# One decoder step on one core: the first norm taken tile by tile, the cached keys requested at the end of wv, and the second norm's weights applied where the gathered blocks leave PSUM

## The chip, the core and the metric

One core of a Trainium2 chip runs the whole program. The metric is the device time of one execution in microseconds. Engines are named as in the profile: PE (matrix), PEld (its weight loads), DVE (vector), ACT (scalar), POOL (GpSimd) and SP (which here only issues DMAs).

## The reference, cut to what matters

576 tokens (512 of a prompt, 64 sampled ones, 8 rows in each of 8 sequences) go through one layer with D = 1024.

```python
xn = rmsnorm(x, norm1_g)              # x * rsqrt(mean(x*x) + eps) * g
proj = xn @ w_in                      # u, v | rwkv r,k,v,w,a,g | q | 3 gates
mk_p, mv_p = mem_prompt @ xa_wk, mem_prompt @ xa_wv     # prompt's keys, values
o_xa = mem_attend(q, keys, values)    # samples use cache_mem_k, cache_mem_v
merged = sum over b of sigmoid(gate_b) * (o_b @ w_branch[b])
h = x + merged @ w_out
h = h + hier_moe(rmsnorm(h, norm2_g), ...)   # 32 experts, 2 for each token
y = rmsnorm(h, final_g)
# hier_moe: logits from the normed rows; expert(x) = (silu(x @ wg) * (x @ wu)) @ wd
```

The second norm's weight g multiplies column d of a row. It can be applied to the row at any place before the expert's first product, since the expert sees x * rstd * g.

## The kernel before, in words

Tokens lie in five tiles `TILES`: four of 128 rows and one of 64. Float32 products are made of three fp32r products: high times high, low times high, high times low.

**First norm (lines 1329 to 1343, 1963 to 1993, 2325 to 2351).** For each tile t ACT squares and sums the row and takes the root (`root(t)`), DVE takes the reciprocal and scales the row by it and by g (`normed(t)`, step "xn"), PE turns the tile in two halves of four 128x128 transposes (L1336), ACT copies each half out of PSUM as the high part (`high(t)`, L1977) and DVE subtracts it from PSUM for the low part (`rest(t)`, L2336). PE starts when `consts_ready` is set, which POOL does after all its constants (L2776). ACT and DVE take roots 0, 1, 2 first, then the high and low parts of tiles 0 and 1 between the roots of 3 and 4, then those of tile 2, then the weights of projection unit 0 (ACT makes their high part at L1960, DVE their low part at L2317, `upto(1, split)`), then tiles 3 and 4. PE waits for the last low part and for the unit's low weights, and then runs unit 0.

**Projection units.** `unit_plan` lists 45 units of weights: 7 "rwkv" units of 256 columns (0 to 6), u, v, q, wk, wv (15 and 16), 24 "merge" units and 4 "out" units (two of 512 output columns c, in two halves of the depth). SP loads each through a ring of four slots (`load_unit`); ACT and DVE split it in order. For a rwkv unit PE makes four parts: two blocks m of 128 output channels by two column ranges of tokens, 0 to 255 and 256 to 575; each part is 24 matmuls (L1412 to L1414). Between the first and the second part of unit 0 PE turns the previous rows (`shift_in`, L1384), which DVE copies out before it splits units 1 and 2.

**Queue of SP at the start (lines 1129 to 1149).** x tile 0, g1b (norm weights), x tiles 1, 2, 3, x tile 4, weights of unit 0, then the small tables and units 1 to 3.

**Cached keys (lines 1186 to 1210, 1827 to 1876).** SP, after the last wv unit has been evacuated by ACT, stores the prompt's values, loads unit 20, g2b (the second norm's weights on all partitions, 512 KB), seven small tables of the router, and then the 8 cached key blocks and 8 value blocks of 512 KB each through the six buffers `kvs`. PE turns the keys of block 0 (`turn_keys(0)`, L1836) after the probabilities of prompt tile 3 have been turned.

**The out stage and the router (lines 636 to 724, 793 to 917).** As DVE adds each tile's output to h (L707), ACT squares it (L666), PE turns it (L645) and makes the router's logits (L652). After the last h of half c, DVE multiplies h by g2b into x2 (`scaled(c)`, L697 and L699). At the end of the second half it does so before it takes the logits (L851). ACT scales x2 by rstd (L800) and stores it as `normed_tokens` (`x2_stored`). DVE then ranks the logits and writes `sel` (L886); PE counts places (L734, L736) and makes the lists (L744), with dummy products (`idle_products`, L620) between: 30 after the logits, 6 and 28 further on. POOL gathers each expert's rows by `il` (L980).

**The experts (lines 727 to 792, 809 to 935).** 32 experts, 64 rows each. For expert e PE turns the gathered block (`turn_in`, L751), ACT copies it to xs (L813), PE makes gate and up (L625, L626), ACT takes silu (L820), DVE multiplies (L924, "h"), PE turns that (`turn_h`, L778), DVE copies it (L934, "ht"), PE makes the down product (L632), DVE copies y (L929) and POOL scatters it (L989). PE's order is: gate_up(e), turn_in(e+1), down(e-1), turn_h(e). Each expert has 6 MB of weights in three slots of a ring of nine. SP's order is fixed: experts 0 and 1 and the gate weights of expert 2 as the out stage ends, the up weights of expert 2 (L589) after `x2_stored`, its down weights (L593) after the first two gathers, then each slot as an expert of three before has used it ("gh", "gu", "d").

## Time and profile before

| what | value |
|---|---|
| median of 3 runs | 1334.75 us (1333.68 to 1335.48) |
| the profiled execution, its own time | 1330.63 us |
| its span, first to last instruction | 1328.9 us |
| PE busy | 1184.9 us (89%) |
| PEld busy | 874.3 us (66%) |
| DVE, ACT, POOL busy | 410.0, 328.9, 92.8 us |
| mean granted TensorE clock | 0.961 |
| DMA moved | 283.80 MB |

The profiled execution is one of its own: 4.1 us under the median. Times of the trace are counted from the span's start. In the rows below a timeline line gives start, duration, engine, line, operation, written tile<-read tiles, count, and in brackets the engine's idle time before it with what ended it. Consecutive instructions of one line are merged, with their count.

### The profile page before, as it was taken

What the parts mean: (1) busy time and instruction counts of PE and PEld (TensorE: products, weight loads), DVE (VectorE), ACT (ScalarE), POOL (GpSimd) and SP (SyncE); (2) the same over time, 40 slices, a digit from 0 to 9 for tenths busy, and PEclk for the clock granted to TensorE, in tenths of its full rate; (3) what the DMA queues carried; (4) which work ended last, traced back from release to release, by engine and by line L of the source; (5) the groups of instructions that cost most, each with busy time, mean ns of one, the idle gap of its engine ahead of it and who ended that gap; (6) DMA issues with size and microseconds to landing.
All of it is one profiled execution on the core that took longest, in us unless ns stands there. A gap on an engine that the chain in (4) does not pass through costs nothing. (4 is left out here: it accounts for less than half of the span.)

```text
span 1328.9 us, 23704 instructions
## 1 busy us (share of the span) xinstructions
PE 1184.9 (89%) x10532; PEld 874.3 (66%) x10532; DVE 410.0 (31%) x705; ACT 328.9 (25%) x550; POOL 92.8 (7%) x132
## 2 busy tenths in 40 slices
PE   3999999999999989999999998999887778888870
PEld 3989998987789879999999877333332223333330
DVE  4336632243345534424233314111111111111116
ACT  5445232332432424223232313111000000010002
POOL 3000000000100010000000001111111111111100
PEclk8999989999899999999999999999999999998995
DMA  7110104000232572323232838999999999999976
GB/s 232 64 33 1 34 5 154 11 4 5 65 126 68 144 226 80 96 72 96 72 92 99 311 130 327 420 419 418 419 419 419 419 420 419 420 420 419 418 325 218
DMA packets 113281, 283.80 MB, mean 214 GB/s; under 512 B 23507, under 2 KB 70821, under 8 KB 88602
## 3 DMA queue, kind: packets, MB, share of 16 engines
q1 hardware_dynamic: 107402, 270.45, 53.9%
q0 software_dynamic: 5120, 9.46, 1.9%
q10 hardware_dynamic: 656, 2.36, 0.4%
q8 instruction: 84, 1.38, 0.4%
q14 instruction: 19, 0.16, 0.0%
HBM read 273.96 MB, written 15.60 MB: 218 GB/s over the span
## 5 line engine op out<-in xcount | busy, mean ns | idle before, releaser
L625 PE MATMUL bank<-slot,xs 128*64 128x512 f32 x512 | 248.6, 634 | 65.6 <-DMA slot<-in_e_wu_dram 64.4
L626 PE MATMUL bank<-slot,xs 128*64 128x512 f32 x512 | 249.8, 637 | 0.0
L625 PEld LDWEIGHTS bank<-slot,xs 128*64 128x64 f32 x512 | 69.7, 145 | 208.7 <-issue 207.2
L1243 PE MATMUL bank<-xnh,wh 128*128 128x256 f32 (+1 forms) x448 | 133.1, 297 | 0.6 <-DVE mt L2718 0.6
L1245 PE MATMUL bank<-xnh,low 128*128 128x256 f32 (+1 forms) x448 | 132.6, 296 | 0.0
L1244 PE MATMUL bank<-xnl,wh 128*128 128x256 f32 (+1 forms) x448 | 132.6, 296 | 0.0
L820 ACT ACTIVATE sg<-bank 64x512 f32<-64x512 f32 x32 | 19.0, 594 | 422.4 <-PE bank L626 422.4
L924 DVE TENSOR_TENSOR h<-sg,bank 64x512 f32<-64x512 f32 x32 | 21.7, 679 | 327.0 <-ACT sg L820 327.0
L632 PE MATMUL bank<-slot,ht 128*64 128x512 f32 x512 | 117.0, 598 | 0.5 <-DVE ht L934 0.5
L2317 DVE TENSOR_TENSOR low<-ring,wh 128x1536 fp32r<-128x1536 f32 (+1 forms) x45 | 89.9, 2005 | 84.4 <-ACT wh L1960 77.0
L1243 PEld LDWEIGHTS bank<-xnh,wh 128*128 128x128 f32 x448 | 85.0, 190 | 1.3 <-issue 1.2
L1960 ACT ACTIVATE wh<-ring 128x1536 fp32r<-128x1536 f32 (+1 forms) x45 | 75.4, 1682 | 41.3 <-PE bank L1294 20.8
L1244 PEld LDWEIGHTS bank<-xnl,wh 128*128 128x128 f32 x448 | 85.0, 190 | 0.0
L1245 PEld LDWEIGHTS bank<-xnh,low 128*128 128x128 f32 x448 | 85.0, 190 | 0.0
L632 PEld LDWEIGHTS bank<-slot,ht 128*64 128x64 f32 x512 | 34.1, 136 | 59.7 <-issue 50.2
L1412 PE MATMUL bank<-xnh,wh 128*128 128x256 f32 (+1 forms) x224 | 69.2, 309 | 4.2 <-DVE xnl L2336 4.2
L626 PEld LDWEIGHTS bank<-slot,xs 128*64 128x64 f32 x512 | 69.7, 145 | 0.0
L1413 PE MATMUL bank<-xnl,wh 128*128 128x256 f32 (+1 forms) x224 | 67.6, 302 | 0.0
L1414 PE MATMUL bank<-xnh,low 128*128 128x256 f32 (+1 forms) x224 | 67.5, 301 | 0.0
L1476 PE MATMUL bank<-sx 64*64 64x64 f32 x672 | 58.4, 227 | 7.4 <-issue 5.0
L1476 PEld LDWEIGHTS bank<-sx 64*64 64x64 f32 x672 | 55.5, 140 | 8.6 <-issue 6.0
L989 POOL DMA_INDIRECT expert_outputs<-yo,il x32 | 32.5, 1015 | 394.6 <-DVE ht L934 390.8
(477 smaller groups left out, 2230.9 us busy)
## 6 DMA issues: line engine op xcount, KB each, us to landing
slot<-in_e_wg_dram SPq DMA_DIRECT2D x64, 1024.0 KB, 28.4
slot<-in_e_wu_dram SPq DMA_DIRECT2D x64, 1024.0 KB, 28.0
slot<-in_e_wd_dram SPq DMA_DIRECT2D x64, 1024.0 KB, 28.7
ring<-in_w_in_dram SPq DMA_DIRECT2D x13, 1024.0 KB, 8.6
ring<-in_w_in_dram SPq DMA_DIRECT2D x24, 512.0 KB, 4.2
ring<-in_w_branch_dram SPq DMA_DIRECT2D x24, 256.0 KB, 4.7
kvs<-in_cache_mem_k_dram SPq DMA_DIRECT2D x8, 512.0 KB, 5.6
kvs<-in_cache_mem_v_dram SPq DMA_DIRECT2D x8, 512.0 KB, 4.4
```

Source lines behind the costliest of these rows:

```text
L625: pe.matmul(out[64:128, :], tok, wg[:, FF * k:FF * k + FF], start=(k == 0), stop=(k == KD - 1))
L626: mm = pe.matmul(out[0:64, :], tok, wu[:, FF * k:FF * k + FF], start=(k == 0), stop=(k == KD - 1))
L632: mm = pe.matmul(out[64 * c:64 * c + 64, :], hidden[:, f, :], wd[:, D * f + 512 * c:D * f + 512 * c + 512], start=(f == 0), stop=(f == 3))
L1243: pe.matmul(part, w_h, xh_(k, cols), start=(k == 0), stop=False)
L1244: pe.matmul(part, w_h, xl_(k, cols), start=False, stop=False)
L1245: mm = pe.matmul(part, w_l, xh_(k, cols), start=False, stop=(k == nk - 1))
L1412: pe.matmul(part, whi[:, w_], xnh[:, k, cols], start=(k == 0), stop=False)
L1413: pe.matmul(part, whi[:, w_], xnl[:, k, cols], start=False, stop=False)
L1414: mm = pe.matmul(part, wlo[:, w_], xnh[:, k, cols], start=False, stop=(k == KD - 1))
L1476: mm = pe.matmul(head2(2 * a, q, b), t[q, 1, b, :], t[q, 2, b, :], start=True, stop=True)
L1960: act.activation(unit_high(u), unit_raw(u), ACT.Copy).then_inc(hi_ready, 1)
L2317: dve.tensor_tensor(unit_low(u), unit_raw(u), unit_high(u).bitcast(F32), ALU.subtract)\
```

## The change

1. SP's queue at the start: unit 0's weights are asked for after x tile 2, ahead of x tiles 3 and 4. PE's transposes wait for a semaphore `ident_ready`, set as soon as POOL has made the identity. ACT's and DVE's orders take the high and low part of a tile one tile behind its root; unit 0 is split after tile 1. PE turns tiles 0 to 2, makes the two parts of unit 0 that need only tokens 0 to 255 (part m = 0, then turns tile 3, then m = 1, then turns tile 4), and the other two parts after the last low part, with `shift_in` between those.
2. The first four cached key blocks are asked for as soon as the last wv product is done, ahead of the store of the values, unit 20, and the small tables.
3. `scaled` is gone, g2b too. ACT scales h itself into x2. The weights g2x (128x2x4, two DMAs of 16-byte rows) multiply the gathered, turned block as it leaves PSUM, on DVE in place of ACT's copy; DVE does this for expert e+1 before it multiplies "h" of expert e. The branch for experts with over 64 rows is changed alike; it isn't entered here.

The diff, cut to its core:

```diff
-        act_n1 = Steps(... ("sq", 0) ... ("root", 2)] + both("hi", 0) + [("sq", 3), ("root", 3)] + both("hi", 1) ...
+        act_n1 = Steps(... ("root", 1)] + both("hi", 0) + [("sq", 2), ("root", 2)] + both("hi", 1) + [("sq", 3), ("root", 3)] ...
+        TURN_BANK = [0, 1, 2, 3, 4, 5, 6, 4, 5, 6]
...
-            def scaled(c):
-                dve_o.wait(dve, ("h", c, 4))
-                g = g2b[:, cols]
-                for m in range(2):
-                    dve.tensor_tensor(x2[:, 2 * m:2 * m + 2, cols], h[:, 2 * m:2 * m + 2, cols],
-                                      g.unsqueeze(1).to_broadcast([128, 2, 512]), ALU.mult)
-                dve_o.done(dve.tensor_tensor(x2[0:NS, 4, cols], h[0:NS, 4, cols], g[0:NS, :], ALU.mult), ("x2", c))
...
-                scaled(c)
...
             def gate_up(e):
-                act_e.wait(pe, ("xs", e))
+                dve_e.wait(pe, ("xs", e))
...
-            dve_o.wait(act, ("x2", OUTS - 1))
+            dve_o.wait(act, ("h", OUTS - 1, 4))
...
-                act_t.done(act.activation(x2[0:tn, t, :], x2[0:tn, t, :], ACT.Identity, scale=rstd[0:tn, t:t + 1]), ("x2", t))
+                act_t.done(act.activation(x2[0:tn, t, :], h[0:tn, t, :], ACT.Identity, scale=rstd[0:tn, t:t + 1]), ("x2", t))
...
-                act_e.done(act.activation(xs[e % 2][:, :, :], psum[2][:, :].rearrange("p (c n) -> p c n", n=128), ACT.Copy), ("xs", e))
...
+            def normed(to):
+                return dve.tensor_tensor(to[:, :, :].rearrange("p c (f n) -> p c f n", n=CAP),
+                                         psum[2][:, :].rearrange("p (c f n) -> p c f n", c=4, n=CAP),
+                                         g2x[:, :, :].rearrange("p f c -> p c f").unsqueeze(3).to_broadcast([128, 4, 2, CAP]), ALU.mult)
+
+            def evacuate(e):
+                pe_m.wait(dve, ("t", e))
+                if e >= 2:
+                    pe_m.wait(dve, ("gu", e - 2))
+                dve_e.done(normed(xs[e % 2]), ("xs", e))
+
+            evacuate(0)
             for e in range(EX + 1):
+                if e + 1 < EX:
+                    evacuate(e + 1)
                 if e < EX:
                     act_e.wait(dve, ("silu", e))
...
+                elif t == 2:
+                    load_units(0)
             sp.dma_start(x_sb[0:NS, 4, :], x_sample.rearrange("b t d -> (b t) d")).then_inc(x_loaded[4], 16)
-            load_units(0)
...
+            sp.wait_ge(unit_used, first_unit["wv"] + 2)
+            for n in range(4):
+                load_cache(n)
             act_evac.wait(sp, first_unit["wv"] + 1)
             store(mem_v_out[0, 0].rearrange("(m p) h d -> p m (h d)", p=128), vn[:, :, :])
             load_units(20)
-            sp.dma_start(g2b[:, :], norm2_g.to_broadcast([128, D])).then_inc(g2_loaded, 16)
+            for f in range(2):
+                sp.dma_start(g2x[:, f, :], norm2_g[0:1, 512 * f:512 * f + 512].rearrange("a (p c) -> (a p) c", c=4)).then_inc(g2_loaded, 16)
...
-            for n in range(2 * DB):
+            for n in range(4, 2 * DB):
...
-            pe.wait_ge(consts_ready, 1)
+            pe.wait_ge(ident_ready, 1)
+            for t in range(3):
+                turn_tile(t)
+            dve_n1.wait(pe, ("lo", 1, 1))
+            pe.wait_ge(lo_ready, 1)
+            rwkv_part(0, 0, 0)
+            turn_tile(3)
+            rwkv_part(0, 1, 0)
+            turn_tile(4)
             pe.wait_ge(par_loaded, 16 * 11)
...
             dve_n1.wait(pe, ("lo", 4, 1))
+            pe.wait_ge(consts_ready, 1)
...
-                if (u, n) == (0, 0):
+                if (u, n) == (0, 1):
                     shift_in()
...
+                    for n in range(2) if u else (1,):
+                        mm = rwkv_part(u, m, n)
...
-            for t in (0, 1, 2):
-                root(t)
-            for t in (3, 4):
-                high(t - 3)
-                root(t)
-            high(2)
-            upto(1, split)
-            for t in (3, 4):
-                high(t)
+            root(0)
+            root(1)
+            high(0)
+            root(2)
+            high(1)
+            upto(1, split)
+            root(3)
+            high(2)
+            root(4)
+            high(3)
+            high(4)
```

DVE's order is changed in the same way: normed 0, 1, rest 0, normed 2, rest 1, split of unit 0, normed 3, rest 2, normed 4, rest 3, rest 4. `rwkv_part(u, m, n)` holds the 24 matmuls of one part as before; `turn_tile(t)` the eight transposes of a tile, in the banks of TURN_BANK.

## Rows read from the trace of the kernel before

**Rows 1.** The page, part 2: busy tenths in 40 equal slices of the span

```profile
PE   3999999999999989999999998999887778888870
DMA  7110104000232572323232838999999999999976
```

**Rows 2.** Timeline of the first 45 us: ACT, DVE and PE

```profile
6.80 1.28 DVE L2329 SCALAR_TENSOR_TENSOR x_sb<-x_sb,rstd,g1b 128x1024 f32<-128x1024 f32 x1
7.91 1.06 ACT L1969 ACTIVATE xq<-x_sb 128x1024 f32<-128x1024 f32 x1 [1.59 <-DMA x_sb<-in_x_prompt_dram]
9.29 1.04 ACT L1969 ACTIVATE xq<-x_sb 128x1024 f32<-128x1024 f32 x1
13.80 4.24 PE L1336 MATMUL bank<-ident,x_sb 128*128 128x128 f32 x24 [13.80 <-POOL restart L2776]
14.95 0.60 ACT L1977 ACTIVATE xnh<-bank 128x512 fp32r<-128x512 f32 x1 [4.20 <-PE bank L1336]
20.96 1.91 ACT L1960 ACTIVATE wh<-ring 128x2048 fp32r<-128x2048 f32 x1
22.99 2.27 DVE L2317 TENSOR_TENSOR low<-ring,wh 128x2048 fp32r<-128x2048 f32 x1
27.18 0.58 PE L1412 MATMUL bank<-xnh,wh 128*128 128x256 f32 x1 [4.18 <-DVE xnl L2336]
31.64 1.03 PE L1384 MATMUL bank<-ident,shn 8*128 8x8 f32 x14
32.60 0.42 PE L1412 MATMUL bank<-xnh,wh 128*128 128x320 f32 x1
33.95 4.49 DVE L2317 TENSOR_TENSOR low<-ring,wh 128x2048 fp32r<-128x2048 f32 x2
...
42.62 0.28 PE L1412 MATMUL bank<-xnh,wh 128*128 128x256 f32 x1
```

**Rows 3.** DMA issues from 4.1 to 4.3 us (unit 0's weights): count, KB, us to landing

```profile
ring<-in_w_in_dram SPq DMA_DIRECT2D x1, 1024.0 KB, 12.2
```

**Rows 4.** PE's transposes of x_sb by stretch: us, busy (count), PEclk, DMA share, GB/s

```profile
14.30:14.80 0.50, 0.50 (x4) 1.00 1.15 283
16.80:17.30 0.50, 0.50 (x7) 1.00 1.05 320
```

**Rows 5.** All engines by stretch: PE, PEld, DVE, ACT, POOL busy, PEclk, DMA share, GB/s

```profile
28.00:30.00 2.00, 2.00 (x11) 2.00 (x11) 0.00 (x0) 2.00 (x2) 0.00 (x0) 0.50 0.01 0
...
812.00:813.00 1.00, 1.00 (x8) 1.00 (x6) 0.00 (x0) 0.00 (x0) 0.00 (x0) 0.51 1.06 434
824.00:825.00 1.00, 0.63 (x4) 0.44 (x4) 0.00 (x0) 0.33 (x1) 0.00 (x0) 1.00 0.00 0
```

**Rows 6.** Timeline of PE and SP around the cached keys

```profile
455.67 1.89 PE L1811 MATMUL bank<-ktm,o_xa 128*128 128x256 f32 x8
...
467.98 8.90 SPq L1210 DMA_DIRECT2D kvs<-in_cache_mem_k_dram  x8
...
472.58 1.09 PE L1836 MATMUL bank<-ident,kvs 128*128 128x128 f32 x8 [2.96 <-DMA kvs<-in_cache_mem_k_dram]
```

**Rows 7.** Timeline from the end of the out stage to the first gather

```profile
798.47 1.67 PE L652 MATMUL bank<-wr,hT 128*128 128x36 f32 x16
810.95 0.59 PE L734 MATMUL bank<-sel,before 128*128 128x192 f32 x2 [3.92 <-DVE sel L886]
...
798.89 2.35 DVE L697 TENSOR_TENSOR x<-h,g2b 128x1024 f32<-128x1024 f32 x2
...
802.15 0.30 DVE L851 TENSOR_TENSOR lg<-lg,bank 128x144 f32<-128x144 f32 x1
...
819.07 1.25 POOL L980 DMA_INDIRECT xg<-normed_tokens,il  x1 [19.91 <-DVE pg L909]
```

**Rows 8.** Timeline of the experts: PE's down product and DVE's product beside it

```profile
842.13 3.65 PE L632 MATMUL bank<-slot,ht 128*64 128x512 f32 x16
...
842.19 0.68 DVE L924 TENSOR_TENSOR h<-sg,bank 64x512 f32<-64x512 f32 x1 [7.23 <-ACT sg L820]
```

More of the change, by code:

```diff
@@ L550, in build @@
                                       ("sq", 4), ("ht", 4)]])
[L551 to L552 removed]
+        dve_o = Steps(sem("dve_o"), ["wr"] + [x for c in range(OUTS) for x in [("h", c, t) for t in range(5)] + ([("lg", c)] if c < OUTS - 1 else [])])
         pe_t = Steps(sem("pe_t"), ["pos", "lists"])
@@ L785, in moe_pe @@
                 if e + 1 < EX:
-                    act_e.wait(pe, ("xs", e))
+                    dve_e.wait(pe, ("xs", e))
                     turn_in(e + 1)
@@ L1043, in general_act @@
                         r = MORE * e + j
-                        pe_n.wait(act, "t", r)
-                        act_n.done(act.activation(xs[0][:, :, :], psum[2][:, :].rearrange("p (c n) -> p c n", n=128), ACT.Copy), "xs")
                         pe_n.wait(act, "gu", r)
@@ L1326, in units_of, with turn_tile, rwkv_part @@
                         unit(u)
-            pe.wait_ge(consts_ready, 1)
-            for n, (t, g) in enumerate(TG):
+            def turn_tile(t):
                 dve_n1.wait(pe, ("xn", t))
-                if n >= 7:
-                    dve_n1.wait(pe, ("lo", *TG[n - 7]))
-                tn = TILES[t][1]
-                for k in range(4):
-                    mm = pe.transpose(psum[n % 7][:, 128 * k:128 * k + tn],
-                                      x_sb[0:tn, t, 512 * g + 128 * k:512 * g + 128 * k + 128], ident[0:tn, 0:tn])
-                pe_n1.done(mm, ("turned", t, g))
+                t0, tn = TILES[t]
+                for g in range(2):
+                    n = 2 * t + g
+                    if n >= 7:
+                        dve_n1.wait(pe, ("lo", *TG[n - 3]))
+                    for k in range(4):
+                        mm = pe.transpose(psum[TURN_BANK[n]][:, 128 * k:128 * k + tn],
+                                          x_sb[0:tn, t, 512 * g + 128 * k:512 * g + 128 * k + 128], ident[0:tn, 0:tn])
+                    pe_n1.done(mm, ("turned", t, g))
+            PARTS = (slice(0, 256), slice(256, NT))
+            def rwkv_part(u, m, n):
+                whi, wlo = wh[:, u % 3, :], low[:, u % 4, :]
+                cols = PARTS[n]
+                part = rwkv_pair(u, m)[:, n, 0:cols.stop - cols.start]
+                for k in range(KD):
+                    w_ = slice(256 * k + 128 * m, 256 * k + 128 * m + 128)
+                    pe.matmul(part, whi[:, w_], xnh[:, k, cols], start=(k == 0), stop=False)
+                    pe.matmul(part, whi[:, w_], xnl[:, k, cols], start=False, stop=False)
+                    mm = pe.matmul(part, wlo[:, w_], xnh[:, k, cols], start=False, stop=(k == KD - 1))
+                return mm
+            pe.wait_ge(ident_ready, 1)
[7 more added lines that the diff above has]
+            turn_tile(4)
             pe.wait_ge(par_loaded, 16 * 11)
@@ L1402, in _ @@
                 pe.wait_ge(lo_ready, u + 1)
-                whi, wlo = wh[:, u % 3, :], low[:, u % 4, :]
                 for m in range(2):
@@ L2336, in rest @@
                     dve_n1.done(dve.tensor_tensor(xnl[:, 4 * g:4 * g + 4, t0:t0 + tn],
-                                                  psum[(2 * t + g) % 7][:, :].rearrange("p (k n) -> p k n", n=128)[:, :, 0:tn],
+                                                  psum[TURN_BANK[2 * t + g]][:, :].rearrange("p (k n) -> p k n", n=128)[:, :, 0:tn],
                                                   xnh[:, 4 * g:4 * g + 4, t0:t0 + tn].bitcast(F32), ALU.subtract), ("lo", t, g))
-            for t in (0, 1, 2):
-                normed(t)
-            for t in (3, 4):
-                rest(t - 3)
-                normed(t)
+            normed(0)
+            normed(1)
+            rest(0)
+            normed(2)
+            rest(1)
+            upto(1, split)
+            normed(3)
             rest(2)
-            upto(1, split)
-            for t in (3, 4):
-                rest(t)
+            normed(4)
+            rest(3)
+            rest(4)
             act_n1.wait(dve, "par")
@@ L2751, in _ @@
             seq(pool.memset(ident[:, :], 0.0))
-            select(ident[:, :], [[-1, 128]], 0, 1, ALU.not_equal, 1.0)
+            pool.affine_select(out=ident[:, :], in_=ident[:, :], compare_op=ALU.not_equal, fill=1.0, base=0, pattern=[[-1, 128]],
+                               channel_multiplier=1).then_inc(ident_ready, 1)
             seq(pool.memset(i64[:, :], 0.0))
```

61 lines of the change are left out of this document (24 added, 37 removed).

## The prediction

> **What bounds the kernel now.** I read the page's slices first. PE is busy nearly without a break from the second slice to the 24th (800 us), and in these slices the DMA line stands mostly at 0 to 5; from the 26th slice (830 us) it is the other way round, DMA at 9 and PE soon at 7 or 8 [rows 1]. So up to the end of the out stage every microsecond of idle PE is one of the total; in the expert stage the weights' stream sets the pace, and what counts is when that stream runs without a pause and how much of the tail follows it. A change can gain in three places: before PE's first product, in a hole of PE before 800 us, and between the end of PE's stage and the full stream. The change touches one of each.
>
> Then I read the timelines of these places. At the start PE waits 13.80 us for POOL's last constant though the first normed tile is there at 6.80 + 1.28 = 8.08; it turns tiles, waits again 4.18 us for the last low part, and starts unit 0 at 27.18 [rows 2]. Around the cached keys PE has one hole of 2.96 us, ended by the landing of the first key block [rows 6]. At the turn to the experts DVE takes the logits at 802.15, though PE has them at 798.47 + 1.67 = 800.14: the multiplication by the norm's weights (2.35 us for the four full tiles, from 798.89) stands between. PE then idles 3.92 us for `sel`, and the first gather goes out at 819.07 [rows 7].
>
> **The start.** SP asks for unit 0's weights before x tiles 3 and 4, so they land no later than the 4.15 + 12.2 = 16.35 us of before [rows 3]; with 0.75 MB fewer ahead I take 12 to 14. ACT's new chain in order: square and root of tile 1 from 7.91 (a tile takes 1.4, from one square at 7.91 to the next at 9.29) to 9.4; high part of tile 0, two times 0.60, which finds PE's transposes just done (they need 14.95 - 13.80 = 1.15 to the first half, now from 8.1); tile 2's root to about 12.2; high part of tile 1 to 13.4; high part of unit 0, 1.91, to 15.4. DVE's low part of unit 0 takes 2.27, to about 17.8 [rows 2]. DVE's own norms and low parts fit in between: a norm is 1.28.
>
> PE starts part 0 there. The part has 24 matmuls. On the fast clock the last three parts of unit 0 took 42.62 - 32.60 = 10.0 for 320 + 256 + 320 columns, so one of 256 takes 2.9 and one of 320 takes 3.6. On the slow clock it takes about 4.5: the first part took 31.64 - 27.18 = 4.46, most of it at granted clock 0.50 (1.2 GHz) [rows 2, 5]. I take slow for the first and fast for the second. So: 17.8 + 4.5 = 22.3, tile 3's eight transposes 1.4 (a third of 4.24), second part 2.9 to 26.6, tile 4 and the tables' transposes 1.2 (estimate from the same row), the last high and low parts 1.1: PE is free to go on at 28.9. What is left is 3.6 + 1.03 (`shift_in`) + 3.6 = 8.2 against 42.62 - 27.18 = 15.4 from the old start. Unit 0 ends at 37.1 instead of 42.6: **5.5 us less**. Moved instructions cost nothing beyond that: SP issues the same DMAs, POOL nothing new.
>
> What is late next is unit 1's low part. It is ready 33.95 + 4.49/2 = 36.2, so 3.5 after the end of `shift_in` at 32.67 [rows 2]; now only one part of 3.6 lies behind `shift_in`. A tie: 0 to 0.2.
>
> The ends: with unit 0's weights no earlier than 16.35, the low part comes at 20.7, 2.9 later, and the gain is 2.6; with both parts on the fast clock PE goes on at 27.0 and the gain is 7.4 (1.6 more from part 0, the rest from faster transposes).
>
> Which clock? The granted clock stands at 1.00 from the first instant, before any PE work, but the pace tells otherwise: PE does 4 transposes in half a microsecond at 14.3 and 7 at 16.8 [rows 4]. So it began slow and sped up while it ran nothing but transposes. In the new order the transposes come in three bursts with pauses, which is why I take slow for the part behind them. The Trainium skill, TensorE: Matmul & The Clock Gate (PE-mode transpose), says that transposes don't count as busy for the clock. Rows 4 speak against that for these ones. By that rule the first part is slow for certain (5.5); by rows 4 it may be fast (7.4).
>
> **The cached keys.** They are asked for at 467.98 and land 4.6 later, at 472.58 less the hand-over; PE was ready 2.96 earlier, at 469.6 [rows 6]. Now they are asked for when the last wv product ends, about 455.8 (the scores that follow it start at 455.67), and land at 460 to 462 with the other three: 8 us of slack, and unit 20 and the small tables, which now go behind 2 MB, aren't used for 20 us and more. Blocks 4 and up still wait for steps of PE that move with it. **2.9 us less**; between 2.5, if the copies of the first turned keys are late by some tenths, and 2.96. Two tiny loads in place of one of 512 KB: nothing, SP has time there.
>
> **The turn to the experts.** Without `scaled`, DVE takes the logits at 800.2 instead of 802.15: 1.95 less, not the whole 3 us, because PE's logits are then late next. `scaled` of the first half lies beside PE's work and is worth 0. `sel` comes 1.95 earlier, and PE's 30 dummy products are done before (807.0), so PE idles 1.97 instead of 3.92 [rows 7]. After the long idle time the granted clock fell to 0.51 at 812 [rows 5], and PE's matmuls for places and lists run in that stretch. If it doesn't fall any more, the chain to the gather gains about 1.0 again (estimate: some 0.4 in the counting products and 0.6 in the six dummy products that then end before DVE). Both are about as likely; I take the middle, 2.5. The gather also needs `x2_stored`. ACT starts on x2 2.3 earlier, but these writes share the DMA with expert weights, so I expect them 1 to 2 earlier, which is enough. Against it stands the copy of the gathered block, 0.60 on ACT for 128x512 [rows 2], now on DVE: nearest row 0.68 for 512 columns with a PSUM operand [rows 8]; 0.1 once, at expert 0. **2.4 us less**; ends 0 (below) and 2.9.
>
> That the stream of weights gives this on to the end: DMA moves nothing at 824 to 825 [rows 5], so it waits for this chain and there is idle time to remove.
>
> In each expert DVE now does the block for e+1 before "h" of e. Waiting behind it: h, and PE's `turn_h`. Before, h was ready at 842.19 + 0.68 = 842.9 and PE's down product held until 842.13 + 3.65 = 845.8 [rows 8]: 2.9 of cover for 0.7. Only expert 0 has no down product before; it is late by 0.7, behind the first releases of slots, and costs nothing while the stream has work queued. Without that cover it would cost 0.7 once.
>
> **Sum.** 5.5 + 2.9 + 2.4 = 10.8. The profiled execution took 1330.63, so it would be 1319.8; it lies 4.1 under the median. I take the same 10.8 off the median: 1334.75 - 10.8 = 1324.0.
>
> **Rivals.**
> A. Unit 0's weights come as late as before, because their small rows and not their place set the landing. The start gives 2.6, the total 7.9: 1326.9. For it: they took 12.2 us for 1 MB. Against: 0.75 MB and more of x went ahead. 0.17.
> B. The turn to the experts gives nothing, because x2's writes and the weights already fill the DMA (share 1.06 at 812) and the first gather waits for `x2_stored`. Total 8.4: 1326.4. Against: DMA at 0.00 at 824. 0.10.
> C. The clock is kept in both places. 7.4 + 2.9 + 2.9 = 13.2: 1321.6. For it: rows 4. 0.16.
> D. Slower. DVE's product with the broadcast weights in a 4-level pattern takes far over 0.7. From 2.9 on it stalls PE at `turn_h` in every expert; PE has, at 7 to 8 tenths busy, some 3 us of waiting in each expert to give away. So it decides from about 6 us, and from 6.4 on (31 experts by 0.4) the gain is eaten and the kernel is slower by over 0.2%, at 1338 for 6.45. No row has such a price. 0.02.
> E. Two of the three parts are worth nothing, for instance by a new wait of PE for unit 1's low part and a late `x2_stored`; a total under 2.7. 0.05. That the change doesn't do what it says belongs here: the experts' stage is shortened by 3 us on DVE in the text, but only 2 can count.
>
> The forecast itself has 0.50. About 0.2% (2.7 us) is what a measurement of this kernel can tell from no change. All but D and E are faster: 0.93, same 0.05, slower 0.02. The range goes from C, with 1 us for the spread of medians, to A and B together (5.5 less): 1320.5 to 1329.2.
>
> **What would show it.** Right: part 0 starts near 18 us and unit 1 near 37; no hole before L1836, which starts near 464 (472.6 less 5.5 and 2.9); L851 right behind the logits; the hole before L734 near 2 us; DMA full some 10 to 11 us earlier; DVE's new product at 0.7. Wrong: unit 0's high part waiting for a DMA after 14 us; a wait of PE for unit 1; a gather that waits for `x2_stored`; a hole in the DMA share around experts 1 to 3.

## The result, and the profile after

The changed kernel takes 1322.46 us (median of 4 runs, 1321.68 to 1323.27); the kernel before, run beside it, takes 1335.12 (1333.68 to 1335.73). The ratio is 0.9913, 95% interval [0.99, 0.9925]: 12.7 us less. The profiled execution took 1323.27 with a span of 1321.5, so it is 7.4 shorter than the profiled execution of before, which was one of the short ones. A second set on another chip gave 0.9925 [0.9912, 0.9939], 9.8 us less by the medians.

Part 2 of the page of the changed kernel, busy tenths in 40 slices, against [rows 1]:

```profile
PE   6999998999999999999999997999877888878870
DMA  7210105000322662232323758999999999999976
```

The first slice of PE went from 3 to 6. At the other end the DMA line looks as it did: the stream of the weights has its 9 in the same slices of a shorter span.

The start, from the timeline of the changed kernel (start us, us, engine, line, operation, and in brackets the idle time before it with what ended it), against [rows 2]:

```profile
8.16 1.94 PE L1341 MATMUL bank<-ident,x_sb 128*128 128x128 f32 x8 [8.16 <-DVE x_sb L2354]
13.37 1.90 ACT L1983 ACTIVATE wh<-ring 128x2048 fp32r<-128x2048 f32 x1
15.31 2.29 DVE L2342 TENSOR_TENSOR low<-ring,wh 128x2048 fp32r<-128x2048 f32 x1 [0.50 <-ACT wh L1983]
17.75 0.55 PE L1353 MATMUL bank<-xnh,wh 128*128 128x256 f32 x1 [2.10 <-DVE low L2342]
20.23 0.41 PE L1355 MATMUL bank<-xnh,low 128*128 128x256 f32 x1
21.98 1.03 PE L1341 MATMUL bank<-ident,x_sb 128*128 128x128 f32 x8
27.54 0.41 PE L1353 MATMUL bank<-xnh,wh 128*128 128x320 f32 x1 [0.65 <-DVE xnl L2361]
35.91 0.39 PE L1353 MATMUL bank<-xnh,wh 128*128 128x256 f32 x1
```

Part 0 starts at 17.75 (17.8 was forecast). ACT takes the weights at 13.37 with no wait for a DMA: they are there. Part 0 is slow up to 20.45 (a product every 0.21 us) and fast from then on (every 0.12). The granted clock in the rows of this stretch reads 1.00 throughout, so slow and fast are told here by the pace of the products. Unit 1 starts at 35.91 instead of 42.62.

The cached keys, same timeline, against [rows 6]:

```profile
449.62 1.89 PE L1834 MATMUL bank<-ktm,o_xa 128*128 128x256 f32 x8
449.82 1.91 SPq L1187 DMA_DIRECT2D kvs<-in_cache_mem_k_dram  x4
463.41 1.04 PE L1859 MATMUL bank<-ident,kvs 128*128 128x128 f32 x8
```

They are asked for at 449.82, the hole is gone, and PE turns them 9.17 us earlier than before, 6.05 of which were there already at the scores (455.67 to 449.62).

The turn to the experts, same timeline, against [rows 7]:

```profile
788.75 1.67 PE L652 MATMUL bank<-wr,hT 128*128 128x36 f32 x16
790.51 0.30 DVE L832 TENSOR_TENSOR lg<-lg,bank 128x144 f32<-128x144 f32 x1 [0.59 <-PE bank L652]
799.31 0.59 PE L724 MATMUL bank<-sel,before 128*128 128x192 f32 x2 [1.99 <-DVE sel L867]
805.20 0.80 SPq L576 DMA_DIRECT2D slot<-in_e_wu_dram  x2
806.75 1.25 POOL L975 DMA_INDIRECT xg<-normed_tokens,il  x1 [17.31 <-DVE pg L890]
814.40 0.75 PE L741 MATMUL bank<-ident,xg 128*128 128x128 f32 x4 [3.19 <-DMA xg<-normed_tokens,il]
815.18 0.69 DVE L901 TENSOR_TENSOR xs<-bank,g2x 128x512 f32<-128x512 f32 x1 [7.74 <-PE bank L741]
821.32 0.33 SPq L576 DMA_DIRECT2D slot<-in_e_wg_dram  x1
```

Up to the gather all goes as intended. In this text a time counted from the logits is counted from the start of the last row of sixteen logits' products (788.75 here, 798.47 in the kernel before). That row comes 9.72 earlier than before; DVE takes the logits 0.09 behind its end (790.42); the gather goes out at 806.75, so 12.32 earlier: the chain gained 2.60. Then it is lost. PE waits 3.19 for the gathered block and turns it at 814.40; in the kernel before this was at 823.88, so only 9.48 are left. And from the logits to the first slot that SP may fill again it is 821.32 - 788.75 = 32.57 us, where the kernel before needs 829.01 - 798.47 = 30.54: 2 us more. What that is worth at the end is taken up with the experiments.

The stretches of the changed kernel (PE, PEld, DVE, ACT, POOL busy with counts, PEclk, DMA share, GB/s), against [rows 5]:

```profile
804.00:806.00 2.00, 2.00 (x31) 1.86 (x30) 0.70 (x4) 0.00 (x0) 0.00 (x0) 1.00 0.04 14
806.00:812.00 6.00, 5.21 (x47) 5.02 (x45) 1.24 (x9) 1.49 (x2) 2.25 (x2) 1.00 0.98 362
813.00:815.00 2.00, 0.60 (x4) 0.56 (x4) 0.00 (x0) 0.00 (x0) 0.00 (x0) 1.00 0.03 12
816.00:819.60 3.60, 3.60 (x10) 1.10 (x12) 0.00 (x0) 0.00 (x0) 0.92 (x1) 0.53 0.92 380
```

The clock no longer falls where it fell before [rows 5]; it falls now behind the wait for the gathered block, and the first half of expert 0's gate and up products runs at 1.2 GHz (granted clock 0.53). While the gather is under way the DMA is full (0.98), and it stands idle before and behind that (0.04 and 0.03). What fills it are the up weights of expert 2, which SP asked for 1.55 us before the gather, in the row of 805.20. They are two DMAs of 1 MB, so 2 MB; the expectations below call this load, and that of the gate weights, 1 MB, which is half of it. In the kernel before, SP asked for them at 814.86, 4.21 before the gather.

The DMA issues of this stretch, changed kernel first, then the kernel before (count, KB each, median us from issue to landing; the gather is the first one alone):

```profile
normed_tokens<-x ACTq DMA_DIRECT2D x4, 512.0 KB, 9.8
xg<-normed_tokens,il POOLq DMA_INDIRECT x1, 7.6
```

```profile
normed_tokens<-x ACTq DMA_DIRECT2D x4, 512.0 KB, 7.4
xg<-normed_tokens,il POOLq DMA_INDIRECT x1, 4.8
```

ACT starts on the normed tokens 1.21 us behind the start of the logits' last row (789.96) and not 3.68 behind it (802.15), but their writes take 2.4 longer beside the same weights, so SP's up weights go out 16.45 us behind the logits, as before (16.39). The chain to the gather moved, the weights ahead of it did not.

Behind the first release something else is new. PE waits for expert 0's `h`, its multiplication on DVE, first in the changed kernel, then in the one before (PE's timeline):

```profile
826.76 0.69 PE L768 MATMUL bank<-ident,h 64*128 64x64 f32 x4 [1.37 <-DVE h L919]
```

```profile
833.81 0.69 PE L778 MATMUL bank<-ident,h 64*128 64x64 f32 x4 [0.73 <-DVE h L924]
```

DVE does the block of expert 1 first, so `h` comes 0.64 later, and expert 1 releases its first slot 9.76 behind expert 0's (at 831.08) and not 9.11. Twice the DMA runs dry before the weights that a release allows are under way: its share is 0.46 in 821.75 to 822.75 and 0.66 in 833.75 to 834.75. The kernel before has no such place in the same stretch.

### The profile page after: what moved, and what is told of

Read it like the earlier page. It is cut to its first block and busy times, and to the rows that moved or that the text cites. A ratio compares the mean times of both kernels' runs of the same rounds, so it can differ in the third digit from the quotient of the medians.

```text
span 1321.5 us, 23698 instructions
## 1 busy us (share of the span) xinstructions
PE 1184.7 (90%) x10532; PEld 874.2 (66%) x10532; DVE 423.4 (32%) x731; ACT 310.3 (23%) x518; POOL 93.3 (7%) x132
## 5 line engine op out<-in xcount | busy, mean ns | idle before, releaser
L901 DVE TENSOR_TENSOR xs<-bank,g2x 128x512 f32<-128x512 f32 x32 | 22.1, 692 | 322.1 <-PE bank L741 322.1
```

## The experiments

Executions of one kernel differ by up to some 4 us to either side of their median, so each kernel was timed in 5 to 12 executions beside the kernel before, and the profiled execution of each was read by stages. The table gives the length of each stage in us, each the difference of two starts in the timelines: *start* is the first product of unit 1; *middle* goes from there to the first turned probabilities; *to keys* to the first turned keys; *behind keys* to the last turned probabilities of the cached part; then the out stage, up to the logits, is 291.30 to 291.33 in all and is left out; *routing* goes on to the issue of the first gather; *block* to the first slot that SP fills again; *stream* to the first load of the tail. The last column is the sum of the three before it.

| kernel | start | middle | to keys | behind keys | routing | block | stream | last three |
|---|---|---|---|---|---|---|---|---|
| before | 42.62 | 414.78 | 15.18 | 34.56 | 20.60 | 9.94 | 471.82 | 502.36 |
| before again | 43.17 | 416.10 | 15.99 | 36.01 | 21.44 | 9.71 | 471.81 | 502.96 |
| start only | 36.88 | 416.75 | 16.24 | 36.18 | 20.53 | 10.45 | 471.85 | 502.83 |
| keys only | 43.52 | 416.87 | 12.06 | 34.40 | 20.81 | 10.18 | 471.88 | 502.87 |
| second norm only | 43.75 | 416.95 | 14.39 | 34.22 | 19.23 | 13.19 | 471.66 | 504.08 |
| keys' hole filled | 42.98 | 419.40 | 16.00 | 34.37 | 22.04 | 9.67 | 472.29 | 504.00 |
| changed | 35.91 | 415.44 | 12.06 | 34.04 | 18.00 | 14.57 | 472.39 | 504.96 |
| changed again | 37.05 | 417.19 | 12.06 | 33.88 | 18.00 | 14.31 | 472.33 | 504.64 |
| parts 1 and 2 | 37.39 | 414.03 | 12.07 | 33.60 | 20.58 | 10.51 | 471.77 | 502.86 |
| gather first | 36.03 | 415.03 | 12.06 | 34.10 | 18.01 | 9.42 | 477.27 | 504.70 |
| 42 dummies | 36.05 | 415.53 | 12.06 | 33.49 | 19.16 | 12.54 | 472.03 | 503.73 |
| gate weights later | 37.23 | 414.10 | 12.07 | 33.62 | 18.01 | 14.50 | 471.27 | 503.78 |
| the same, more dummies | 36.87 | 417.09 | 12.07 | 33.91 | 18.01 | 14.11 | 471.74 | 503.86 |
| weights behind gather | 35.96 | 415.41 | 12.06 | 33.81 | 20.55 | 14.59 | 472.09 | 507.23 |

**The start alone**: the kernel before with the pieces of the diff on `act_n1`, `dve_n1`, `TURN_BANK`, `ident_ready`, `load_units(0)`, `turn_tile` and `rwkv_part`.

> Part 1 alone (the first norm tile by tile). Theory: all of the start's gain is made before unit 1, whose first product starts at 35.9 us instead of 42.6, and about 0.7 of it is given back before the cached keys, as the profile of the whole change shows; the rest reaches the end. About 6.0 us less: ratio 0.9955. Rival: the gain is worth more than the profile shows (the medians of the two kernels lie 12.7 apart, the profiled executions 7.4), then this part is at 8 or more, ratio under 0.994.

Measured: 1327.71 us (6 runs), ratio 0.9941 [0.992, 0.9962]. Unit 1 starts at 36.88; the hole before the keys is still there. PE's timeline at the keys:

```profile
469.87 1.96 PE L1857 MATMUL bank<-ident,kvs 128*128 128x128 f32 x8 [4.01 <-DMA kvs<-in_cache_mem_k_dram]
471.62 2.77 PE L1864 MATMUL bank<-prt,vn 128*128 128x128 f32 x16
```

The hole is 4.01 and not 2.96, and behind it eight transposes take 1.96 us and sixteen products 2.77: the clock fell in the hole (granted clock 0.52 in the first microsecond behind it, 0.50 in the next two). In the profiled execution of the kernel before it had not (1.00 there, and 1.09 for the transposes [rows 6]).

**The keys alone**:

```diff
+            sp.wait_ge(unit_used, first_unit["wv"] + 2)
+            for n in range(4):
+                load_cache(n)
             act_evac.wait(sp, first_unit["wv"] + 1)
...
-            for n in range(2 * DB):
+            for n in range(4, 2 * DB):
```

> Part 2 alone (the first four cached key blocks asked for at wv's end). Theory: PE's hole of 2.96 before L1836 goes, and 0.1 to 0.5 of the wait for the last value block with it: 3.1 us less, ratio 0.9977. Rival: the time goes into a later wait, ratio within 0.0005 of 1.

Measured: 1328.85 (6 runs), ratio 0.9953 [0.9936, 0.9969]: some 6 us less, at least 4, where 2.9 was forecast. The profile shows no hole and fast transposes:

```profile
472.45 1.04 PE L1841 MATMUL bank<-ident,kvs 128*128 128x128 f32 x8
```

**The second norm alone**: the remaining pieces of the diff (`g2x`, `normed`, `evacuate` on DVE, `scaled` gone).

> Part 3 alone (the second norm's weights at the evacuation). Theory from the profile of the whole change: the logits are taken 2.0 earlier and the gather goes out 2.6 earlier, but it lands late, since the up weights of expert 2 go out just before it; the first expert starts no earlier, on a slow clock, and the weights' stream is full 2 us later than it could be. The kernel is 0 to 2 us slower, ratio 1.000 to 1.0015. Rival from the medians: what is left of 12.7 after 6.0 and 3.1 is this part's, so 3 us faster, ratio 0.9975, and the late gather is seen in this one profile alone.

Measured: 1334.02 (12 runs), ratio 0.9994 [0.9981, 1.0007]: no gain that can be seen. The interval goes from 2.5 us less to 0.9 more, so by the timed runs alone neither the 2.4 of the prediction is ruled out nor a small loss. Timeline of this kernel (PE, SP, POOL):

```profile
817.14 0.80 SPq L575 DMA_DIRECT2D slot<-in_e_wu_dram  x2
819.86 1.25 POOL L974 DMA_INDIRECT xg<-normed_tokens,il  x1 [18.55 <-DVE pg L889]
826.12 0.75 PE L740 MATMUL bank<-ident,xg 128*128 128x128 f32 x4 [1.80 <-DMA xg<-normed_tokens,il]
```

The same picture with nothing else changed: the up weights stand 2.72 ahead of the gather, a new hole of 1.80 stands before the block, and from the logits to the first release it takes 19.23 + 13.19 = 32.42.

**The kernel before once more**, as a measure of what an execution differs by.

> The kernel before, unchanged, profiled and timed once more. Theory: the profiled execution of before (1330.6) was one of the shortest that this kernel has, and most take 1334 to 1336; then this profile shows 3 to 5 us more in a place that can be named, most likely the landing of the first gathers and the clock behind it. Rival: a profiled execution is always some 4 us shorter than the others; then this one is near 1331 too, with the same times at all places.

Measured: 1333.11 (12 runs), ratio 0.9994 [0.9979, 1.0008]. PE at the keys in this execution:

```profile
475.26 1.78 PE L1836 MATMUL bank<-ident,kvs 128*128 128x128 f32 x8 [3.76 <-DMA kvs<-in_cache_mem_k_dram]
```

Here too the clock fell in the hole (granted clock 0.62, then 0.50). Of the four profiled executions with the late keys and an open hole, the clock fell in the two with holes of 3.76 and 4.01 and stayed in the two with 2.96 and 2.16. By the table the late keys cost (15.45 - 12.06) + (35.24 - 33.87) = 4.8 us on average, from these four against the nine with early keys. By these profiles it is 4.8 that part 2 gives, not the 2.96 of one execution.

**The keys' hole filled**, to see whether the second half of that cost is the clock. The keys stay late:

```diff
             def turn_keys(b):
+                if b == 0:
+                    act_x.wait(pe, ("p", 3))
+                    for _ in range(26):
+                        pe.transpose(psum[SKT_BANK[0]][:, 0:128], ident[:, :], ident[:, :])
                 pe.wait_ge(kv_loaded[b % KVS], 16 * (b // KVS + 1))
```

> The kernel before with 26 dummy transposes of the identity in the hole ahead of the first turned keys; the keys are asked for as late as before. Theory (in most executions of the kernel before the hole is 3.5 to 4 us, and the clock falls in it, which costs 1.5 to 2 us more than the hole): PE has almost no idle time ahead of the keys, the eight transposes take 1.1 us instead of 1.8, the sixteen products behind them 1.95 instead of 2.94, and the total is 1 to 2 us below the kernel before: about 0.9988. Rival (the hole alone is the cost): 1.000, and the transposes behind it are as slow as they were.

PE's timeline of this kernel at the keys:

```profile
474.44 3.00 PE L1831 MATMUL bank<-ident 128*128 128x128 f32 x26
478.38 1.09 PE L1840 MATMUL bank<-ident,kvs 128*128 128x128 f32 x8 [0.94 <-DMA kvs<-in_cache_mem_k_dram]
```

In the profile it does what was expected: 16.00 to the keys, so the hole without the dummies would be 3.9, and the transposes take 1.09. *Behind keys* is 34.37, not the 36.0 of the two executions with a slow stretch. In the medians nothing is seen of it: 1333.98 (11 runs), ratio 1.0001 [0.9992, 1.001], where 0.9988 was expected. So the fall in the hole is shown in traces, and its price of 1.6 when it happens; that it happens in most executions is not borne out. By the interval the clock's part is at most 1.1 us, so the late keys cost 3.4 to 4.5 in the median by this run, and at least 4.1 by the run with the keys alone; the table's average is 4.8. The price stays open to that extent.

**The changed kernel again**, beside the next runs.

> The changed kernel again, beside the next three on the same chip. Both theories: 0.9905 of the kernel before (12 to 13 us less); the first gathered block lands 7 to 8 us after it is asked for, the transposes of the gathered block wait some 3 us for it, the first half of the first expert's gate and up products runs at 0.85 us for a pair instead of 0.43, and the first slot is released some 14.5 us after the gather was asked for.

Measured: 1324.22 (5 runs), 0.9925 [0.9912, 0.9939]. The gather is followed by the turned block 7.43 later, after a wait of 2.96, and by the first release 14.31 later; all as before.

**The gather ahead of the weights**:

```diff
             dve_t.wait(sp, "lg")
             sp.wait_ge(x2_stored, 80)
-            load(2, 1)
             dve_t.wait(sp, "c12")
             for n in range(2):
                 sp.wait_ge(gathered[n], 16)
+            load(2, 1)
             load(2, 2)
```

> The changed kernel with the up weights of expert 2 asked for only behind the landing of the first two gathers. Theory (the gather is late because 1 MB of weights was queued 1.5 us ahead of it): it lands 4 to 5 us after it is asked for, so 3 us earlier; PE's wait for it (3.2) is gone, the clock does not fall, and the first slot is released 3 to 4.5 us earlier than in the changed kernel. The total: 2 to 4 us less than the changed kernel if the weights' stream passes this on; 0 if the 1 MB that now starts later is missed, which would be seen as a wait of PE for the weights of expert 2. Rival (the gather is slow by itself: small rows, normed_tokens written just before): it still takes 7 us, nothing gained, and the 1 MB asked for 8 us later makes it 1 to 3 us slower.

The timeline of this kernel (POOL, PE, SP) from the gather on:

```profile
806.54 1.25 POOL L975 DMA_INDIRECT xg<-normed_tokens,il  x1 [17.32 <-DVE pg L890]
810.84 0.64 PE L741 MATMUL bank<-ident,xg 128*128 128x128 f32 x4
811.61 0.81 SPq L576 DMA_DIRECT2D slot<-in_e_wu_dram  x2
815.96 0.33 SPq L576 DMA_DIRECT2D slot<-in_e_wg_dram  x1
```

The first half holds entirely: with no weights beside it the gather lands 3.5 us after its issue and is turned at 4.30, without a wait, and the first slot is released 9.42 after the issue, 5.1 earlier than in the changed kernel. The second half does not: the median is 1324.70, 0.9937 [0.9923, 0.9951], nothing gained. The stretches say why. First the changed kernel, from the logits to the first release, the 14 us behind it, and the first 50 us behind the logits; then the same of this one, then of the kernel before (columns as above):

```profile
788.75:821.32 32.57, 26.07 (x220) 21.31 (x220) 14.24 (x90) 9.00 (x13) 3.77 (x4) 0.95 0.84 327
821.32:835.32 14.00, 12.63 (x62) 4.94 (x60) 1.83 (x4) 1.19 (x2) 1.00 (x1) 1.00 0.92 349
788.75:838.75 50.00, 42.13 (x295) 27.20 (x293) 17.22 (x95) 10.19 (x15) 4.77 (x5) 0.97 0.87 339
```

```profile
788.53:815.96 27.43, 24.11 (x220) 20.82 (x220) 14.25 (x90) 9.00 (x13) 3.78 (x4) 1.00 0.72 276
815.96:829.96 14.00, 12.63 (x54) 4.58 (x52) 1.70 (x3) 0.59 (x1) 1.00 (x1) 0.88 1.01 421
788.53:838.53 50.00, 45.31 (x312) 28.63 (x312) 18.26 (x97) 10.19 (x15) 6.38 (x7) 0.97 0.85 341
```

```profile
798.47:829.01 30.54, 25.93 (x220) 22.53 (x220) 16.25 (x92) 9.59 (x14) 3.77 (x4) 0.94 0.84 321
829.01:843.01 14.00, 13.27 (x64) 5.08 (x62) 1.78 (x3) 2.38 (x4) 1.00 (x1) 1.00 1.02 423
798.47:848.47 50.00, 44.66 (x308) 29.65 (x308) 19.07 (x97) 11.97 (x18) 5.79 (x6) 0.97 0.91 360
```

Time by rate gives the bytes. From the logits to the tail all three move some 202.5 MB, and from 50 us on all run at 408 GB/s, so what counts is what the first 50 us moved: 339 by 50 = 17.0 MB in the changed kernel, 17.1 with the gather first, 18.0 before. The missing 1 MB is 2.5 us at 408 GB/s; by the last column of the table the changed kernel is 2.6 longer than the kernel before and the one with the gather first 2.3. The two lose it at different places. With the gather first the DMA is idle ahead of the first release (27.43 by 0.28 = 7.7 us, against 32.57 by 0.16 = 5.2 in the changed kernel) and full behind it (421). In the changed kernel it runs dry behind the release (349). So a release that came 5 us earlier gave nothing, because 2.5 us more of idle DMA were paid for it.

This holds for all fourteen profiles. From 50 us behind the logits on they run at 408 or 409 GB/s, and the bytes of the first 50 us order their last columns: 17.5 to 18.0 MB in the six with the old second norm (502.36 to 504.00 us), 17.0 to 17.3 in the seven others that end at 503.73 to 504.96, and 15.9 in the last kernel of the table (507.23).

**More dummy products** in the wait for the block (28 to 42 in `moe_pe`).

> The changed kernel with 42 instead of 28 dummy products ahead of the first gathered block. Theory (PE's idle 3.2 us ahead of the block make the clock fall, and the first half of the first expert's products pays 1.7 us for it): PE is busy until about 813, no pair of products takes 0.85, the first slot is released 1.7 us earlier, and the total is 1 to 1.7 us less than the changed kernel. Rival (the pace of these products does not count, since the stream is set by the landing of weights already under way): the first release comes earlier but the total is the same within 0.5.

Measured: 1322.07 (5 runs, 1318.08 to 1323.83), 0.9909 [0.9891, 0.9926], the fastest median and 2.1 below the changed kernel on the same chip, though the intervals overlap. The block's first release is 12.54 behind the gather instead of 14.31, and *last three* is 0.9 to 1.2 shorter. But this profile has slow stretches elsewhere, one ahead of the gather and one behind PE's wait for expert 0's `h` (granted clock 0.50 from 827 to 830). A row of its timeline, and the stretch behind it for the first of them (columns as above):

```profile
799.00 0.76 PE L724 MATMUL bank<-sel,before 128*128 128x192 f32 x2 [1.99 <-DVE sel L867]
```

```profile
800.00:802.00 2.00, 2.00 (x11) 2.00 (x10) 0.12 (x1) 0.00 (x0) 0.00 (x0) 0.50 1.02 418
```

The same idle time of 1.99 before the selection, behind which the changed kernel stayed at 1.00, ended here at 0.50, and the gather came 1.15 later.

**Parts 1 and 2 without the second norm.**

> The start and the keys as changed, the second norm as in the kernel before. By the profiles so far the stretch from the last logits product to the first store of the tail takes 502.4 to 503.0 us with the old second norm and 503.7 to 505.0 with the new one. Theory (the new second norm costs 1.5 us, since the gather now stands behind 1 MB of weights and the clock falls ahead of the first expert): this kernel is 0 to 1.5 us faster than the whole change, 0.990 to 0.9915 of the kernel before, with logits near 788.6, the gather asked for 20.5 later and the first slot released 31 us after the logits. Rival (the second norm is worth the 2.4 us of the prediction): 0.9925 to 0.994, slower than the whole change.

Measured: 1322.84 (6 runs), 0.9925 [0.9906, 0.9943]. By the median this is the changed kernel; the two can't be told apart. The stages of the profiles say that the third part is worth less than nothing: *last three* is 502.86, and over all, six profiles with the old second norm give 502.36 to 504.00 (mean 503.0), three with the new one and nothing else in that stage 504.08 to 504.96 (mean 504.6). The timed runs don't bear 1.6 us out: the interval of the second norm alone ends at 0.9 more. The timeline of this kernel (POOL, PE):

```profile
808.98 1.25 POOL L981 DMA_INDIRECT xg<-normed_tokens,il  x1 [19.89 <-DVE pg L910]
814.36 0.75 PE L752 MATMUL bank<-ident,xg 128*128 128x128 f32 x4 [0.57 <-DMA xg<-normed_tokens,il]
```

The up weights are asked for at 805.37. The gather goes out 2.2 later than in the changed kernel and its block is turned at the same time, 814.36 against 814.40.

**The gate weights of expert 2 behind the normed tokens**, to give their writes the DMA:

```diff
-            load(2, 0)
             dve_t.wait(sp, "lg")
             sp.wait_ge(x2_stored, 80)
+            load(2, 0)
             load(2, 1)
```

> The changed kernel, with the gate weights of expert 2 (1 MB) asked for right ahead of its up weights, so behind the landing of the normed tokens, and not ahead of them. Theory (the stream loses what the DMA stands idle between the landing of the normed tokens and the first slot's release, and the gather is late behind the up weights): the normed tokens land 2 to 3 us earlier, near 12 us after the logits instead of 16.5, both loads are issued there and nearly through when the gather is asked for, the gather lands in 4.5 to 6 us instead of 7.6, the first slot is released 1.5 to 5 us earlier with the rest of the stage as long as before (472 us), and the total is 2 to 4 us below the changed kernel: 0.988 to 0.990. Rival (the stage is set by bytes alone, and idle time of the DMA only moves): 0.9915 to 0.9925 as the changed kernel.

Measured: 1322.28 (6 runs), 0.9916 [0.9896, 0.9936]: as the changed kernel. A DMA issue and a row of the timeline of this kernel:

```profile
normed_tokens<-x ACTq DMA_DIRECT2D x4, 512.0 KB, 4.4
```

```profile
813.94 0.75 PE L741 MATMUL bank<-ident,xg 128*128 128x128 f32 x4 [3.15 <-DMA xg<-normed_tokens,il]
```

The writes do land in 4.4 instead of 9.8, and SP goes on 11.3 us behind the logits. But with 4 MB behind them instead of 2 the DMA is full until past 810, and the gather is late as before, turned 7.61 behind its issue. The expected 4.5 to 6 was wrong.

**The same with more dummies** (40 in the wait for the selection, 34 in that for the block):

> The same as the run before it, with 40 instead of 30 dummy products in the wait for the selection and 34 instead of 28 in the wait for the gather, so that the clock has no hole of 2 us to fall in. If the clock matters here: no stretch at 0.5 between the logits and the second expert, the gather 18.0 us after the logits in every execution, and 0 to 1.5 us less than the run before. If not: the same within 0.5.

Measured: 1322.71 (6 runs), 0.9917 [0.9898, 0.9936], no difference from the run before it. The hole before the selection is filled, but PE still waits 1.4 for the block, and the clock still falls behind it.

**The weights right behind the gather**: in the changed kernel, `load(2, 1)` one line down, behind `dve_t.wait(sp, "c12")`.

> The changed kernel with the up weights of expert 2 asked for at DVE's last step of the routing, some 0.8 us behind the issue of the first gather instead of 1.5 us ahead of it, and not behind its landing as in the run that loaded them behind the gathers. Theory (from the logits to the end the kernel moves the same bytes at the full rate, and what it loses is the idle time of the DMA in between; the gather is late by what was queued ahead of it): the gather lands in 4.3 to 5.2 us, the clock does not fall, the first slot is released 27.5 to 28.5 us after the logits, the rest takes 474 to 475 (472 plus the 1 MB that was not moved before), and logits to tail is 502 to 503 us, where the changed kernel took 504.6 to 505.0. In the median 1.5 to 2.5 us below the changed kernel, 0.989 to 0.9905 of the kernel before, if that much can be seen in it. Rival (idle time before the first release is regained later): logits to tail stays at 504.5.

A stretch of this kernel ahead of the gather (columns as above):

```profile
802.00:804.00 2.00, 2.00 (x10) 2.00 (x11) 1.70 (x3) 0.00 (x0) 0.00 (x0) 0.50 0.82 334
```

Measured: 1323.19 (6 runs), 0.9919 [0.9904, 0.9934]: not faster. In this execution the clock fell behind the 1.99 before the selection and stayed down for some 6 us; the gather came 2.55 later, and the DMA stood idle for it (share 0.00 in 806 to 808). The weights, asked for 0.78 behind the gather, did not leave it alone either: it was turned 6.41 behind its issue, against 4.30 with no weights beside it. Both halves of the theory missed, though the fall of the clock spoiled this execution as a trial of the second: it was the longest of the six.

## Why the prediction was right, and where it was not

The forecast of 1324.0 holds, as does its range, but its three terms (5.5, 2.9, 2.4) were each off and made up for one another; that the total fits so well is in part luck. By the averages of the stages they are 6.6, 4.8 and -1.6: 9.8, the 9.8 of the second set of runs and 2.9 below the first. The timed runs of the parts alone give 7.1, 5.9 and 0.7 by their medians, 13.7 in all, with 1.7 to 2.8 us of uncertainty on each. So the first two terms are clearly gains. Of the third the timed runs say only that it lies between 2.5 less and 0.9 more; the loss of 1.6 is read from profiles alone and lies outside that.

**The start: right, 1.1 too small.** 43.21 (mean of five) to 36.60 (mean of nine). Part 0 started 0.05 us from where it was put, and rival A falls: unit 0's weights were there at 13.37. Part 0 took 4.23, not 4.5. Most of the surplus lies between its end and the second half: PE went on at 27.54, not 28.9, since eight transposes took 0.8 on the fast clock instead of 1.4, and the last low part came earlier. Unit 1's low part was no wait.

Of the clock I had left open whether it would be fast. It was slow through the three bursts of transposes (eight in 1.94 to 1.97) and for the first half of part 0, so the middle value was right and rival C wrong here. The Trainium skill, TensorE: Matmul & The Clock Gate (PE-mode transpose), says that transposes don't count as busy for the clock. Behind bursts with pauses the trace agrees with it as to part 0 (0.21 us for a product up to 20.45), behind the unbroken row of 24 transposes of the kernel before it does not [rows 4]. Nor does it in the run with the hole filled, where 26 transposes ran through most of the hole and the granted clock stayed at 1.00.

**The keys: right in kind, the term mis-sized.** The term of 2.9, "between 2.5 [...] and 2.96", took the size of a hole from one execution as its value in all. The executions have 2.2 to 4.0, and in the longer ones the clock falls and 1.6 more are lost behind the hole. Measured: 3.4 before the keys and 1.4 behind them. The upper end should have been the hole plus the products behind it at half the clock, which was to be had from the profile's own slow stretches [rows 5].

**The turn to the experts: wrong, from 2.4 to -1.6 by the profiles.** Its first steps are right to a tenth: the selection comes 10.56 behind the logits instead of 12.48, so 1.92 less (1.95 was said); PE idles 1.99 (1.97); in the profile the clock stays up as far as the gather, and its issue gains 2.60. The step that failed is "these writes share the DMA with expert weights, so I expect them 1 to 2 earlier, which is enough". They came not at all earlier (16.45 against 16.39), the DMA being full, as rival B had it; and what they release is not only the gather but SP's load of expert 2's up weights. The gather ran up against it: issued 4.21 behind that load it was turned 4.81 later, 3.61 behind it 5.38 (parts 1 and 2), 2.72 behind it 6.26 (second norm only), 1.55 behind it 7.65. Ten profiles have this load alone ahead of the gather, 1.4 to 4.6 us ahead, and the longer the gather is issued behind it, the sooner it lands: 4.4 to 4.5 us after its issue at the far end, 7.4 to 7.6 at the near end, in order but for up to 0.3 us between neighbours. What the chain gained, the gather waited longer, and the longer wait put PE's clock down for the first products of expert 0. I had looked for who waits for the gather's *permission* and not for who is ahead of it on the DMA. Rival B named the right resource, but put its price at nothing, where it is a loss.

There was a second error under it: that an earlier first release is passed on to the end. The run with the gather first shows that it isn't, if the DMA stands idle for it.

**The experts: right but for expert 0.** DVE's product with the broadcast weights takes 0.69 (0.7 was said), and *stream* is 471.3 to 472.4 with it and 471.8 to 472.3 without: D falls. But "costs nothing while the stream has work queued" failed: by the trace the stream had run out of work. PE waits 1.37 for expert 0's `h` and not 0.73, expert 1's releases come 0.65 later, and the DMA runs dry before their weights are under way, the sign that the prediction had named ("a hole in the DMA share around experts 1 to 3"). In the 14 us behind the first release the changed kernel moves (423 - 349) by 14 = 1.0 MB less than the kernel before, and that is about all that it lost: up to the release, 2 us later than before, it had moved as much more (327 by 32.57 = 10.65 MB against 9.80). How the 1.0 MB divides between the 0.65 and the late first release was not tried alone. E falls as well.

## What to carry to other kernels

A hole read from one execution is a sample: price it with what runs behind it at the lower clock, and look at a second execution before taking its size. When a chain that ends in a small DMA is made shorter, look at what its queue neighbours do at the new moment: a transfer that is released by something else and has not moved will now stand in front. And in a stage that moves a fixed number of bytes at the full rate, count the idle time of the DMA up to its last hole, not the time of a release: two kernels whose first release differed by 5 us ended together, one with its hole ahead of the release, the other behind it.

## What the runs showed that was not expected

- The clock behind one and the same idle time is not one and the same. After 1.99 to 2.00 us before the selection it stayed up in four profiles (changed, changed again, gather first, gate weights later: 18.00 to 18.01 from the logits to the gather) and fell in three (second norm only 19.23, 42 dummies 19.16, weights behind gather 20.55), in the last for 6 us at 0.50, with 2.55 us lost up to the gather. Such falls, longer or shorter, are the likeliest source of the 414 to 419 us of the *middle* stage, which none of the edits touch and which makes most of the scatter between executions. By the granted clocks the three shortest (414.0 to 414.8) spend some 27 us of it at 1.2 GHz and the longest (419.4) some 41, an estimate from stretches of 5 us; at half the pace 14 us more at 1.2 GHz would cost 7, and the stage is 5 longer. This was read, not tried.
- The first gather beside 2 MB of weights that were asked for 1.4 to 1.6 us ahead of it lands in 7.4 to 7.6 us and not in 3.5, and still takes 6.4 when it is issued 0.78 us ahead of them.
- The writes of the normed tokens take 7.4 us in the kernel before, 9.8 when they start 2.5 us earlier into the full DMA, and 4.4 when 2 MB of weights are taken from in front of them; where the DMA is full, to start them earlier did not bring them in earlier.
